# Delta-rule inverse: the first four levels on compact 32x32 blocks in four quarters of the array, the fifth as off-diagonal 32-row blocks

## The chip, the core and the metric

One core of a Trainium2 chip runs the whole program in one launch. The metric is device time in microseconds (us). TensorE is called PE in the profile (PEld is its weight load), VectorE DVE, ScalarE ACT, GpSimd POOL, and SyncE, which issues the weight transfers, SP.

## The reference, cut to what matters

The program is a stack of two model blocks over 256 tokens of width 1024: attention, feed-forward, a gated delta-rule layer (GDN), feed-forward, and then a second stack of feed-forward, convolution and pooling layers. The change touches only the GDN layer. For each of its 16 value heads, and each chunk of tokens, the reference solves a unit lower triangular system:

```
m = where(strict, beta[..., :, None] * kk * decay, 0.0)
a = m + eye(C)
sol = triangular_solve(a, rhs, left_side=True, lower=True, unit_diagonal=True)
```

The kernel works in chunks of 128 tokens, so there are two matrices of 128x128 for a head (t = 0 and 1), and it builds their explicit inverses by doubling: from 2x2 blocks on the diagonal to 4x4, 8x8, 16x16, 32x32, 64x64 and 128x128. With X the inverse so far and A the matrix, a level is the product A X, a mask that leaves the identity and the negated blocks below the diagonal, and two more products that apply X to it, one giving the next X and the other its transpose.

## The kernel before, in words

The 16 heads are taken in four turns (`N_TURNS`) of four heads (`GB`). Each engine has its own hand-written program, and they meet at semaphores. The inner order of a turn i is written out in `gdn_pe`: for each of the six levels, `level_pe(i, lv)` and then one or two fill tiles. A fill tile (`gdn_unit_pe`, one of twelve units of the next turn) is a 256-token projection of 24 matmuls, lines L519, L520 and L521, which need nothing of the level. `FILL` gives their number for the six levels: 2, 2, 1, 2, 1, 1. Unit x waits for the convolution of unit x-2 (`g_conv`) and for its own weights split into a high part (`split_hi` on ACT, L476) and a low part (`split_lo` on DVE, L483). The split of unit x is done three units ahead. In the last turn there are no next units, and the fill is one output projection a level (`gdn_out_pe`, L1253, no convolution to wait for).

A level has, for t = 0 and 1: the product p (L1335; L1332 in level 5), the mask on DVE (`level_dve`, L1839; a plain negation, L1835, in level 5), the product xi (L1350), the product ix (L1361; L1358 in level 5), and ACT copies of xi and ix to SBUF (`level_act`, L1576 and L1580; L1583 at level 4, L1586 at level 5). PE issues p for both t, then xi and ix for t = 0, then xi and ix for t = 1. Every block is 64x64 on one of two row halves (`HALVES`), so one t has 4 heads x 2 halves = 8 matmuls. In the trace a float32 matmul has two records, one behind the other in the program, each with a weight load of its own, so such a group of 8 matmuls is 16 records. The two halves use different tiles of the array, rows and columns 0 to 63 and rows and columns 64 to 127. At level 4 xi is done for the upper half alone, and at level 5 p and ix are one tile each.

DVE runs, behind the two masks of a level: the decay arguments (L1771) at level 0; the three taps of the convolution of units 0 and 1 (`taps_conv_dve`, L1747) with a weight split behind each at level 1; the taps of units 2 and 3 and then a split at level 2; a split, the taps of unit 4, a table and a split at level 3; the taps of units 5 and 6 and a split at level 4. ACT runs, behind the four copies of a level, the splits' high parts (L476), and at level 3 first the squares (`qk_squares_act`, L1536) on which PE's `qk_sums_pe` (L1263) waits between fill units 5 and 6.

Before level 0 the starting blocks are made: `unit_lower_dve` masks A into `xb` (L1807, one instruction a half), `pairs_turn_pe` transposes it on PE (L1313, 16 records for a t), and `pairs_act` copies it (L1569). In turn 0 this stands at the end of a prologue in which DVE is the busy engine. Masks and tables lie in `CONSTS`, loaded at the start by two SP transfers. `gdn_clear_dve` clears the lower left quarters of `xt_` on DVE (L1718). `gdn_pool` waits for the gates and sends them through DRAM.

Of the kernel before, what the change touches and what calls it, by code (L numbers as in the profile page):

```python
# [59 lines left out]
for _name, _n in COLS:  # L60
# [5 lines left out]
          ("level", 5 * 64), ("pair_t", 64), ("incl_up_neg", 128), ("strict_up", 128), ("reset", T), ("centre", 128), ("pool_inv", 4 * T)]  # L66
# [53 lines left out]
def build(nc, dram, out_dram):  # L120
    with ExitStack() as ctx:
# [1044 lines left out]
        g_beta = sem("beta_ready")  # L1166
# [31 lines left out]
        x_, ip, xb = gd.cut(2, GB, H), gd.cut(2, GB, H), gd.cut(2, GB, H)  # L1198
# [117 lines left out]
        def level_pe(pe, i, lv):  # L1316

            base = 2 * LEVELS * i + 2 * lv
            for t in range(2):
# [9 lines left out]
                for n in range(GB):  # L1329
                    o = slice(n * H, (n + 1) * H)  # L1330
                    if lv == LEVELS - 1:
                        last = nc.tensor.matmul(ps[HALVES[1], bank, o], a_t[HALVES[0], t, n, HALVES[1]], x_[HALVES[0], t, n], start=True, stop=True)  # L1332
                    else:
                        for r in HALVES:
                            last = nc.tensor.matmul(ps[r, bank, o], a_t[r, t, n, r], x_[r, t, n], start=True, stop=True)  # L1335
                last.then_inc(g_p, 1)
            for t in range(2):
# [9 lines left out]
                if lv < LEVELS - 1:  # L1347
                    for n in range(GB):
                        for r in HALVES[:1] if lv == LEVELS - 2 else HALVES:
                            last = nc.tensor.matmul(ps[r, level_bank(lv, "xi", t), n * H:(n + 1) * H], xb[r, t, n], ip[r, t, n], start=True, stop=True)  # L1350
# [4 lines left out]
                for n in range(GB):  # L1355
                    o = slice(n * H, (n + 1) * H)
                    if lv == LEVELS - 1:
                        last = nc.tensor.matmul(ps[HALVES[0], bank, o], ip[HALVES[1], t, n], xt_[HALVES[1], i % 2, t, n, HALVES[1]], start=True, stop=True)  # L1358
                    else:
                        for r in HALVES:  # L1360
                            last = nc.tensor.matmul(ps[r, bank, o], ip[r, t, n], xb[r, t, n], start=True, stop=True)  # L1361
# [205 lines left out]
        def pairs_act(act, i, t):  # L1567
            act.wait_ge(g_turned, 2 * i + t + 1)
            nc.scalar.activation(flat(x_[:, t]), ps[:, 2 + t, 0:T], ACT.Copy).then_inc(g_x0, 1)  # L1569

        def level_act(act, i, lv, t):
            base = 2 * LEVELS * i + 2 * lv + t + 1
            if lv < LEVELS - 1:
                act.wait_ge(g_xi, 2 * (LEVELS - 1) * i + 2 * lv + t + 1)
                r = HALVES[0] if lv == LEVELS - 2 else slice(0, P)
                nc.scalar.activation(flat(x_[r, t]), ps[r, level_bank(lv, "xi", t), 0:T], ACT.Copy).then_inc(g_x, 1)  # L1576
            act.wait_ge(g_ix, base)
            bank = level_bank(lv, "ix", t)
            if lv < LEVELS - 2:
                last = nc.scalar.activation(flat(xb[:, t]), ps[:, bank, 0:T], ACT.Copy)  # L1580
            elif lv == LEVELS - 2:
                for r in HALVES:
                    last = nc.scalar.activation(xt_[r, i % 2, t, :, r], ps[r, bank, 0:T].rearrange("p (n s) -> p n s", n=GB), ACT.Copy)  # L1583
            else:
                r = HALVES[0]
                last = nc.scalar.activation(xt_[r, i % 2, t, :, HALVES[1]], ps[r, bank, 0:T].rearrange("p (n s) -> p n s", n=GB), ACT.Copy)  # L1586
# [1115 lines left out]
```

## Time and profile before

| what | value |
|---|---|
| median of the runs | 1829.75 us (1829.43 to 1829.8, 3 runs) |
| span of the profiled execution | 1828.1 us, 1.65 us under the median |
| granted TensorE clock | 0.998 of full, mean over the span |
| PE busy | 1792.8 us, 98% |
| DVE busy / ACT busy | 1359.7 us, 74% / 1012.4 us, 55% |
| level loops of the four turns | 375 us to 622 us of the span |

The span is the time from the first to the last instruction; start and end of the launch lie around it. Starts are in us from the span's start. A duration in a matmul row includes the way through the array, so neighbouring matmuls overlap and it is the distance of starts that tells the rate: for n records in a merged row it is about (duration of the row less one duration) / (n - 1).

### The profile page before, as it was taken

How to read it: one execution, taken by the hardware profiler on the slowest of the kernel's cores; microseconds unless marked ns; L12 is line 12 of the kernel's file. 1: busy time of each engine (PE TensorE's matmuls, PEld its weight loads, DVE VectorE, ACT ScalarE, POOL GpSimd, SP SyncE). 2: the span in 40 equal slices, each digit the busy share in tenths (PEclk: the TensorE clock that was granted, in tenths of full speed). 3: DMA queues.
4: the chain of work that ended last, by engine and by line, in shares of the span. 5: the costliest groups of instructions: out<-in, count | busy, mean ns of one | idle time of the engine just before them, and what ended most of it. 6: DMA issues, size and time to landing. Idle time of an engine off the chain costs nothing.

```text
span 1828.1 us, 30994 instructions
## 1 busy us (share of the span) xinstructions
PE 1792.8 (98%) x12370; PEld 1591.7 (87%) x12370; DVE 1359.7 (74%) x2255; ACT 1012.4 (55%) x1687; POOL 83.1 (5%) x161
## 2 busy tenths in 40 slices
PE   7999999999999999999999999999999999999998
PEld 6888889889888888888888888888888888988887
DVE  4758878876765048889888969598979897767665
ACT  3557754766665157664655421655556555466553
POOL 0000000000000000001000100010101010000000
PEclk9999999999999999999999999999999999999999
DMA  5256568433321256559788934588878887436552
GB/s 194 93 186 206 185 204 325 137 120 116 117 94 67 88 181 207 185 194 337 251 287 282 351 140 139 207 303 288 315 257 299 282 310 265 161 126 203 191 190 99
DMA packets 102814, 373.94 MB, mean 205 GB/s; under 512 B 11440, under 2 KB 11600, under 8 KB 102544
## 3 DMA queue, kind: packets, MB, share of 16 engines
q1 hardware_dynamic: 80352, 289.88, 46.0%
q0 software_dynamic: 22320, 82.09, 13.3%
q8 instruction: 98, 1.61, 0.4%
q14 instruction: 44, 0.36, 0.1%
HBM read 370.85 MB, written 1.08 MB: 203 GB/s over the span
## 4 chain that ended last, share of the span: by engine, by line
PE 93%; DVE 3%; ACT 3%; issue 1%; DMA 0%; SPq 0%; DVEq 0%; ACTq 0%
PE ps L512 39%; PE ps L515 21%; PE ps L1978 4%; PE ps L519 3%; PE ps L1253 3%; PE ps L520 3%; PE ps L521 3%; PE ps L603 2%; PE ps L890 2%; PE ps L2004 2%; PE ps L1075 1%; PE ps L1350 1%; PE ps L1361 1%; ACT weights_hi L476 1%; DVE weights_lo L483 1%
## 5 line engine op out<-in xcount | busy, mean ns | idle before, releaser
L483 DVE TENSOR_TENSOR weights_lo<-weight_ring,weights_hi 128x1024 fp32r<-128x1024 f32 x477 | 583.2, 1224 | 158.5 <-ACT weights_hi L476 157.6
L476 ACT ACTIVATE weights_hi<-weight_ring 128x1024 fp32r<-128x1024 f32 x477 | 500.9, 1055 | 196.5 <-PE ps L512 122.3
L512 PE MATMUL ps<-u_halves,weights_hi 128*128 128x512 f32 x2176 | 536.6, 391 | 2.3 <-DVE u_halves L379 1.8
L512 PEld LDWEIGHTS ps<-u_halves,weights_hi 128*128 128x128 f32 x2176 | 400.3, 188 | 83.5 <-DVE u_halves L379 3.4
L515 PE MATMUL ps<-u_halves,weights_lo 128*128 128x256 f32 x2176 | 304.4, 282 | 0.0
L515 PEld LDWEIGHTS ps<-u_halves,weights_lo 128*128 128x128 f32 x2176 | 288.1, 191 | 10.2
L512 PE MATMUL ps<-act_halves,weights_hi 128*128 128x512 f32 x952 | 231.6, 391 | 0.0
L512 PEld LDWEIGHTS ps<-act_halves,weights_hi 128*128 128x128 f32 x952 | 173.4, 188 | 32.8 <-DVE weights_lo L483 0.4
L713 DVE SCALAR_TENSOR_TENSOR ffn_tiles<-ffn_tiles,cond 128x1024 f32<-128x1024 f32 x144 | 175.4, 1220 | 3.5 <-DMA ffn_tiles<-in_ada 3.3
L625 ACT ACTIVATE ffn_tiles<-ps 128x512 f32<-128x512 f32 x136 | 80.8, 594 | 158.2 <-PE ps L515 158.1
L519 PE MATMUL ps<-u_halves,weights_hi 128*128 128x256 f32 x488 | 144.6, 296 | 8.1 <-DVE u L1747 6.1
L515 PEld LDWEIGHTS ps<-act_halves,weights_lo 128*128 128x128 f32 x1088 | 142.3, 191 | 6.4
L515 PE MATMUL ps<-act_halves,weights_lo 128*128 128x256 f32 x1088 | 145.8, 282 | 0.0
L688 DVE TENSOR_TENSOR ffn_tiles<-ps,ffn_tiles 128x512 f32<-128x512 f32 x136 | 93.9, 690 | 64.6 <-ACT ffn_tiles L625 64.5
L520 PE MATMUL ps<-u_halves,weights_hi 128*128 128x256 f32 x488 | 138.7, 284 | 0.0
L521 PE MATMUL ps<-u_halves,weights_lo 128*128 128x256 f32 x488 | 138.5, 284 | 0.0
L799 POOL DMA_DIRECT2D ffn_tiles<-in_ada x144 | 76.1, 529 | 1262.8 <-DVE ffn_tiles L713 798.8
L519 PEld LDWEIGHTS ps<-u_halves,weights_hi 128*128 128x128 f32 x488 | 93.9, 192 | 13.0 <-DVE u L1747 7.0
L260 ACT ACTIVATE u<-h 128x256 f32<-128x256 f32 x88 | 35.6, 411 | 107.6 <-DVE h L739 56.3
L520 PEld LDWEIGHTS ps<-u_halves,weights_hi 128*128 128x128 f32 x488 | 94.0, 193 | 1.1 <-issue 1.0
L521 PEld LDWEIGHTS ps<-u_halves,weights_lo 128*128 128x128 f32 x488 | 94.1, 193 | 0.0
L637 ACT ACTIVATE ffn_tiles<-ffn_tiles 128x256 f32<-128x256 f32 x136 | 56.2, 413 | 27.1 <-DVE ffn_tiles L696 11.8
(280 smaller groups left out, 2105.7 us busy)
## 6 DMA issues: line engine op xcount, KB each, us to landing
weight_ring<-in_w SPq DMA_DIRECT2D x545, 512.0 KB, 4.0
ffn_tiles<-in_ada POOLq DMA_DIRECT2D x144, 512.0 KB, 5.4
scaled<-gates_scratch POOLq DMA_DIRECT2D x8, 512.0 KB, 6.0
arena<-in_alibi POOLq DMA_DIRECT2D x1, 1536.0 KB, 7.1
h<-in_x SPq DMA_DIRECT2D x4, 256.0 KB, 3.9
out<-u SPq DMA_DIRECT2D x4, 256.0 KB, 2.1
consts<-in_consts SPq DMA_DIRECT2D x1, 704.0 KB, 9.8
cond<-in_cond SPq DMA_DIRECT2D x1, 512.0 KB, 10.5
```

The source lines that it names most:

```text
L476: nc.scalar.activation(w_slot(s)[0], ring[:, n % RING], ACT.Copy).then_inc(hi_ready, 1)
L483: nc.vector.tensor_tensor(lo, ring[:, n % RING], hi.bitcast(F32), ALU.subtract).then_inc(lo_ready, 1)
L512: return nc.tensor.matmul(ps[:, bank], hi, halves, start=start, stop=stop, skip_group_check=True)
L515: return nc.tensor.matmul(ps[:, bank, 0:T], lo, halves[:, 0], start=start, stop=stop, skip_group_check=True)
L519: nc.tensor.matmul(out, hi, halves[:, 0], start=start, stop=False)
L520: nc.tensor.matmul(out, hi, halves[:, 1], start=False, stop=False)
L521: return nc.tensor.matmul(out, lo, halves[:, 0], start=False, stop=stop)
L625: nc.scalar.activation(corr[:, f % 2], ps[:, b:b + 2, T:2 * T], ACT.Copy).then_inc(corr_ready, 1)
L688: nc.vector.tensor_tensor(gu[:, f % 3], ps[:, b:b + 2, 0:T], corr[:, f % 2], ALU.add).then_inc(gu_ready, 1)
L713: nc.vector.scalar_tensor_tensor(ada_ring[:, r], ada_ring[:, r], 1.0, cond[:], ALU.mult, ALU.mult, accum_out=mods[:, n:n + 1]).then_inc(ad ...
L799: pool.dma_start(ada_ring[:, n % 3], dram["ada"][n]).then_inc(ada_loaded[n % 3], 16)
L1978: last = nc.tensor.matmul(ps[:, n % 6, 0:T], ring[:, s, k], u[:, k], start=(k == 0), stop=(k == C - 1))
```

## The change

The first four levels (`SMALL`), which only ever fill 32x32 blocks on the diagonal, keep just these: four row quarters (`QUARTERS`) with 32 columns each. Matmuls are 32x32 on 32 columns, four to a head, each on its own quarter of rows and columns of the array. DVE masks and ACT copies of these levels work on 128x128 in place of 128x256. Level 3 has to write its results into the wider layouts, `x64` and `xt_`, quarter by quarter. Level 4 computes only the off-diagonal 32x32 blocks. Level 5 is as before, on the new names `x64` and `ip64`. The clearing goes from DVE to POOL and grows to all of `xt_` and `x64`. The constants shrink by 224 columns.

```diff
-          ("level", 5 * 64), ("pair_t", 64),
+          ("level", 4 * 32), ("pair_t", 32),
...
-        LEVELS, H = 6, 64
+        LEVELS, SMALL, H, Q = 6, 4, 64, 32
+        QUARTERS = tuple(slice(Q * q, Q * q + Q) for q in range(4))
+        UPPER_LOWER = ((QUARTERS[0], QUARTERS[1]), (QUARTERS[2], QUARTERS[3]))
...
 pairs_turn_pe:
-                for r in HALVES:
-                    last = nc.tensor.matmul(ps[r, 2 + t, n * H:(n + 1) * H], xb[r, t, n], ident[r, r], start=True, stop=True)
+                for r in QUARTERS:
+                    last = nc.tensor.matmul(ps[r, 2 + t, n * Q:(n + 1) * Q], xb[r, t, n], ident[r, r], start=True, stop=True)
...
 level_pe, product p:
+                    if lv < SMALL:
+                        for r in QUARTERS:
+                            last = nc.tensor.matmul(ps[r, bank, o], a_t[r, t, n, r], x_[r, t, n], start=True, stop=True)
+                    elif lv == SMALL:
+                        for r0, r1 in UPPER_LOWER:
+                            last = nc.tensor.matmul(ps[r1, bank, o], a_t[r0, t, n, r1], x64[r0, t, n, 0:Q], start=True, stop=True)
...
 level_pe, product xi:
+                        if lv < SMALL:
+                            for r in QUARTERS[:3] if lv == SMALL - 1 else QUARTERS:
+                                last = nc.tensor.matmul(ps[r, bank, o], xb[r, t, n], ip[r, t, n], start=True, stop=True)
+                        else:
+                            r = QUARTERS[1]
+                            last = nc.tensor.matmul(ps[r, bank, o], xt_[r, i % 2, t, n, r], ip[r, t, n], start=True, stop=True)
...
 level_pe, product ix:
+                    if lv < SMALL:
+                        for r in QUARTERS:
+                            last = nc.tensor.matmul(ps[r, bank, o], ip[r, t, n], xb[r, t, n], start=True, stop=True)
+                    elif lv == SMALL:
+                        for r0, r1 in UPPER_LOWER:
+                            last = nc.tensor.matmul(ps[r0, bank, o], ip[r1, t, n], xt_[r1, i % 2, t, n, r1], start=True, stop=True)
...
 level_act:
+            if i == 0 and lv == SMALL - 1 and t == 0:
+                act.wait_ge(g_cleared, 2)
+                if lv < SMALL - 1:
+                    last = nc.scalar.activation(flat(x_[:, t]), ps[:, bank, 0:GB * Q], ACT.Copy)
+                elif lv == SMALL - 1:
+                    for r in QUARTERS[0], QUARTERS[2]:
+                        nc.scalar.activation(x64[r, t, :, 0:Q], heads(r, bank), ACT.Copy)
+                    r = QUARTERS[1]
+                    last = nc.scalar.activation(x64[r, t, :, Q:H], heads(r, bank), ACT.Copy)
+                else:
+                    r = QUARTERS[1]
+                    last = nc.scalar.activation(x64[r, t, :, 0:Q], heads(r, bank), ACT.Copy)
...
+            if lv < SMALL - 1:
+                last = nc.scalar.activation(flat(xb[:, t]), ps[:, bank, 0:GB * Q], ACT.Copy)
+            elif lv == SMALL - 1:
+                for r in QUARTERS:
+                    last = nc.scalar.activation(xt_[r, i % 2, t, :, r], heads(r, bank), ACT.Copy)
+            elif lv == SMALL:
+                for r0, r1 in UPPER_LOWER:
+                    last = nc.scalar.activation(xt_[r0, i % 2, t, :, r1], heads(r0, bank), ACT.Copy)
...
 gdn_clear_dve:
-            for b in range(2):
-                nc.vector.memset(xt_[HALVES[1], b, :, :, HALVES[0]], 0.0)
...
 unit_lower_dve:
-            for r in HALVES:
-                mask = const("pair_t")[r].unsqueeze(1).to_broadcast([H, GB, H])
+            for r in QUARTERS:
+                mask = const("pair_t")[r].unsqueeze(1).to_broadcast([Q, GB, Q])
...
 level_dve:
+            if lv < SMALL:
+                mask = const("level", lv, Q).unsqueeze(1).to_broadcast([P, GB, Q])
+                src = ps[:, bank, 0:GB * Q].rearrange("p (n s) -> p n s", n=GB)
+                last = nc.vector.tensor_tensor(ip[:, t], src, mask, ALU.mult)
+            elif lv == SMALL:
+                for r0, r1 in UPPER_LOWER:
+                    last = nc.vector.tensor_scalar(flat(ip[r1, t]), ps[r1, bank, 0:GB * Q], -1.0, None, ALU.mult)
...
 gdn_pool:
+            pool.wait_ge(root_ready, 3)
+            nc.gpsimd.memset(xt_, 0.0).then_inc(g_cleared, 1)
+            nc.gpsimd.memset(x64, 0.0).then_inc(g_cleared, 1)
```

## Rows read from the trace of the kernel before

**Rows 1.** Windows by stage: busy time of each engine in one turn.

```profile
448.00:518.00 70.00, 68.43 (x910) 62.43 (x907) 47.94 (x85) 45.45 (x82) 1.04 (x2) 1.00 0.34 109
```

**Rows 2.** Waits, 375 to 666 us: who waited for whom, total, times, longest.

```profile
PE ps L519 <- DVE u L1747: 3.2, 3, 1.1
...
PE ps L1350 <- DVE arena L1839: 2.4, 3, 1.9
```

**Rows 3.** Instructions by form, 375 to 622 us: count, busy, mean ns.

```profile
L1839 DVE TENSOR_TENSOR arena<-ps,consts 128x256 f32<-128x256 f32 x40 | 16.7, 424 | 64.7 <-PE ps L1335 64.0
...
L1816 DVE TENSOR_TENSOR arena<-ps,arena 128x512 f32<-128x512 f32 x3 | 2.1, 687 | 0.0
```

**Rows 4.** Timeline of PE, level 1 of turn 1: start, duration.

```profile
455.42 1.15 PE L1335 MATMUL ps<-arena 64*64 64x64 f32 x32
456.63 0.68 PE L1350 MATMUL ps<-arena 64*64 64x64 f32 x16
...
458.64 0.39 PE L519 MATMUL ps<-u_halves,weights_hi 128*128 128x256 f32 x1
```

**Rows 5.** Timeline of DVE, level 1 of turn 1.

```profile
456.15 0.89 DVE L1839 TENSOR_TENSOR arena<-ps,consts 128x256 f32<-128x256 f32 x2 [6.32 <-PE ps L1335]
456.96 1.51 DVE L1747 SCALAR_TENSOR_TENSOR u<-ps,cols,u 128x253 f32<-128x253 f32 x3
460.12 1.23 DVE L483 TENSOR_TENSOR weights_lo<-weight_ring,weights_hi 128x1024 fp32r<-128x1024 f32 x1 [1.66 <-ACT weights_hi L476]
```

**Rows 6.** Timeline of PE, second fill unit of level 1.

```profile
462.83 0.39 PE L519 MATMUL ps<-u_halves,weights_hi 128*128 128x256 f32 x1 [1.06 <-DVE u L1747]
```

**Rows 7.** Timeline of ACT in turn 1: levels 1 and 3, scaled copies behind level 5.

```profile
458.76 0.38 ACT L1580 ACTIVATE arena<-ps 128x256 f32<-128x256 f32 x1
459.04 1.05 ACT L476 ACTIVATE weights_hi<-weight_ring 128x1024 fp32r<-128x1024 f32 x1
...
475.78 1.05 ACT L1536 ACTIVATE gdn_tiles<-mix 128x1024 f32<-128x1024 f32 x1
...
496.40 2.18 ACT L1563 ACTIVATE arena<-ps,arena 128x128 f32<-128x128 f32 x8
```

**Rows 8.** Timeline of PE, levels 4 and 5 of turn 1.

```profile
484.24 0.62 PE L1350 MATMUL ps<-arena 64*64 64x64 f32 x7
484.64 0.27 PE L1361 MATMUL ps<-arena 64*64 64x64 f32 x1
484.70 0.22 PE L1350 MATMUL ps<-arena 64*64 64x64 f32 x1
...
489.31 1.14 PE L1332 MATMUL ps<-arena 64*64 64x64 f32 x16
```

**Rows 9.** Timeline of PE, what of this line runs at 455.43.

```profile
455.42 0.27 PE L1335 MATMUL ps<-arena 64*64 64x64 f32 x2
```

**Rows 10.** Timeline, level 0 of turn 1.

```profile
446.09 1.15 PE L1335 MATMUL ps<-arena 64*64 64x64 f32 x32
446.99 0.75 DVE L1839 TENSOR_TENSOR arena<-ps,consts 128x256 f32<-128x256 f32 x2
```

**Rows 11.** Timeline of PE, level 3 of turn 1.

```profile
472.17 0.33 PE L1335 MATMUL ps<-arena 64*64 64x64 f32 x4
...
478.36 1.88 PE L1263 MATMUL ps<-gdn_tiles,consts 128*128 128x512 f32 x4
```

**Rows 12.** Timeline, end of the prologue, level 0 of turn 0.

```profile
376.52 1.22 DVE L483 TENSOR_TENSOR weights_lo<-weight_ring,weights_hi 128x1024 fp32r<-128x1024 f32 x1 [0.36 <-ACT weights_hi L476]
377.66 0.75 DVE L1839 TENSOR_TENSOR arena<-ps,consts 128x256 f32<-128x256 f32 x2
...
378.13 0.68 PE L1350 MATMUL ps<-arena 64*64 64x64 f32 x16 [1.93 <-DVE arena L1839]
```

**Rows 13.** Timeline of PE, the fill of level 1 in the last turn.

```profile
594.85 3.72 PE L1253 MATMUL ps<-mix,weight_ring 128*128 128x256 f32 x16
```

**Rows 14.** The page, part 3: packets, MB, share of 16 engines.

```profile
q8 instruction: 98, 1.61, 0.4%
```

More of the change, by code:

```diff
@@ L1347, in level_pe @@
                 if lv < LEVELS - 1:
+                    bank = level_bank(lv, "xi", t)
                     for n in range(GB):
-                        for r in HALVES[:1] if lv == LEVELS - 2 else HALVES:
-                            last = nc.tensor.matmul(ps[r, level_bank(lv, "xi", t), n * H:(n + 1) * H], xb[r, t, n], ip[r, t, n], start=True, stop=True)
+                        o = slice(n * Q, (n + 1) * Q)
+                        if lv < SMALL:
[4 more added lines that the diff above has]
+                            last = nc.tensor.matmul(ps[r, bank, o], xt_[r, i % 2, t, n, r], ip[r, t, n], start=True, stop=True)
                     last.then_inc(g_xi, 1)
@@ L1355, in level_pe @@
                 for n in range(GB):
-                    o = slice(n * H, (n + 1) * H)
-                    if lv == LEVELS - 1:
-                        last = nc.tensor.matmul(ps[HALVES[0], bank, o], ip[HALVES[1], t, n], xt_[HALVES[1], i % 2, t, n, HALVES[1]], start=True, stop=True)
-                    else:
-                        for r in HALVES:
-                            last = nc.tensor.matmul(ps[r, bank, o], ip[r, t, n], xb[r, t, n], start=True, stop=True)
+                    o, o64 = slice(n * Q, (n + 1) * Q), slice(n * H, (n + 1) * H)
+                    if lv < SMALL:
[4 more added lines that the diff above has]
+                            last = nc.tensor.matmul(ps[r0, bank, o], ip[r1, t, n], xt_[r1, i % 2, t, n, r1], start=True, stop=True)
+                    else:
+                        last = nc.tensor.matmul(ps[HALVES[0], bank, o64], ip64[HALVES[1], t, n], xt_[HALVES[1], i % 2, t, n, HALVES[1]], start=True, stop=True)
                 last.then_inc(g_ix, 1)
@@ L1577, in level_act @@
+                last.then_inc(g_x, 1)
             act.wait_ge(g_ix, base)
             bank = level_bank(lv, "ix", t)
[L1579 to L1583, printed above, removed]
-            else:
-                r = HALVES[0]
-                last = nc.scalar.activation(xt_[r, i % 2, t, :, HALVES[1]], ps[r, bank, 0:T].rearrange("p (n s) -> p n s", n=GB), ACT.Copy)
+            if lv < SMALL - 1:
[6 more added lines that the diff above has]
+                    last = nc.scalar.activation(xt_[r0, i % 2, t, :, r1], heads(r0, bank), ACT.Copy)
+            else:
+                last = nc.scalar.activation(xt_[HALVES[0], i % 2, t, :, HALVES[1]], heads(HALVES[0], bank, H), ACT.Copy)
@@ L2649, in constant_matrices @@
     put("window_mask", mask)
-    p, q = i % 64, j[:, 0:64]
-    for lv in range(5):
+    p, q = i % 32, j[:, 0:32]
+    for lv in range(4):
         z = 2 ** (lv + 1)
         below = (p // (2 * z) == q // (2 * z)) & (p // z % 2 == 1) & (q // z % 2 == 0)
-        a = CONST["level"][0] + 64 * lv
-        out[:, a:a + 64] = (p == q) * 1.0 - below
+        a = CONST["level"][0] + 32 * lv
+        out[:, a:a + 32] = (p == q) * 1.0 - below
     put("pair_t", (p == q) * 1.0 - ((q == p + 1) & (p % 2 == 0)))
```

29 lines of the change are left out of this document (12 added, 17 removed).

## The prediction

> **What bounds the kernel now.** I read the page first, then the waits of the GDN stretch, then the timelines of one turn, engine by engine. The page gives PE as busy for 98% of the span, and in a turn of 70 us it is busy 68.4 us, with DVE at 47.9 and ACT at 45.5 [rows 1]. PE's own waits are small: 3.2 us in all for the convolution and 2.4 us for a mask [rows 2], while DVE waits 64 us for product p [rows 3]. So time taken from PE's level work comes off the end, as far as the engines that now wait for PE are ready sooner too. That second half decides the size, so I go through the levels by the wait that ends last.
>
> Level 1 of turn 1, with T = 455.42 for its first product [rows 4]: p for both t, 32 records, ends its starts near T+0.93. The masks start at T+0.73 [rows 5]. xi starts at T+1.21, and four groups of 16 records later the fill starts at T+3.22 [rows 4]. The fill does not run free: its second unit waits 1.06 us for the taps of unit 1 and starts at 462.83 [rows 6]. Those taps stand behind a weight split on DVE that starts at 460.12 because it waited for ACT [rows 5], and ACT's L476 starts at 459.04, behind the last level copy at 458.76 [rows 7]. This is a chain from PE's last level product through ACT and DVE back to PE.
>
> **The price of a record.** (1.15 - 0.22) / 31 = 30 ns between starts with two halves in use [rows 4], in the steady part 29. With one tile in use (level 5) it is (1.14 - 0.22) / 15 = 61 ns, 58 without the longer first gap [rows 8]. So the halves really overlap, and each tile is bound by itself. Two records of the two halves start within 10 ns [rows 9], although the program has both records of a matmul one behind the other: the second half's first record passes the first half's second. At level 4 a record of L1361 starts at 484.64, before the last of L1350 at 484.70 [rows 8]; it also passes the two L1361 records of the busy tile. So PE looks past at least three matmuls and the loads between them, not much further: in the seven records before it did not.
>
> A 32x32 record on 32 columns takes about half of 58 ns on its tile, say 32 with the fixed part. A group of one t is now 4 heads x 4 quarters x 2 = 32 records. If all four quarters overlap, a record costs 32/4 = 8 ns; if the look-ahead reaches only three, 32/3 = 10.6. I take 9.5, so a group costs 0.30 us in place of 0.466. The bounds outside are 16 ns (two at a time, 0.51 us a group) and today's 29 ns a record (0.93 us).
>
> **Masks and copies.** 128x256 takes 424 ns and 128x512 687 [rows 3], so 128 columns less save 0.13: a mask takes 0.29. ACT copies of 128 columns start 0.254 us apart ((2.18 - 0.40) / 7) [rows 7], and I take this for 32-row copies as well; between 0.2 and today's 0.38 lies the unknown.
>
> **Level by level**, gain in the start of what follows. Today's first product is complete 0.05 ahead of its mask, at T+0.68; with the group 0.16 shorter it is complete at T+0.51, the mask starts at T+0.56, xi at T+0.91, four groups of 0.30 end, and the fill could start at T+2.25, 0.97 sooner.
> Level 0: DVE comes late anyway, with the mask at T+0.90 [rows 10], so xi gains only 0.13, the groups 0.65: 0.78.
> Level 1: the last product is 0.99 sooner, ACT's last copy 0.11 shorter, and the chain above moves whole: 1.10.
> Level 2: the fill unit needs the taps that follow the masks. The second mask starts 0.30 behind the first, the taps 0.21 behind that (0.34 today, less the 0.13), and three of them take 1.51 [rows 5]: they end at T+0.56+0.30+0.21+1.51 = T+2.58, and with the 0.05 that a semaphore takes the fill starts at T+2.63, not 2.25: 0.59. Here the convolution becomes the bound.
> Level 3: four copies become 14. They start at T+1.43 and take 14 x 0.254 = 3.56, then the squares 1.05 [rows 7], and PE's sums can start at T+6.04. Today they start at 478.36 - 472.17 = 6.19 [rows 11], bound by PE. Gain 0.15 of the 0.97: ACT takes the rest.
> Level 4: two tiles, 16 records at 16 ns, two short DVE instructions a t in place of one. PE alone would gain 0.96, the taps of unit 5 end at T+2.82, gain 0.34.
> Level 5: unchanged. The turned pairs: 2 x (0.466 - 0.304) = 0.32; L1807 becomes four instructions of the new mask's 0.29 where two of the old mask's 0.42 stood, 0.33 us a t, and in turns 1 to 3 fill units hide it.
> A turn in the middle: 0.78 + 1.10 + 0.59 + 0.15 + 0.34 + 0.32 = 3.28, twice 6.56. Turn 0: at the end of the prologue PE waits 1.93 us for the mask [rows 12], DVE gets 0.66 us more of L1807, of which its own wait of 0.36 for ACT takes up about 0.3. So the mask starts 0.35 later, ends 0.13 sooner than that, and with groups 0.65 shorter level 0 gains 0.42 there, and the turn 2.92. The last turn has no convolution: 4 x 0.97 + 0.96 = 4.84, since its fill of 3.65 us from T+2.25 [rows 13] covers the 14 copies, which end at T+4.99. Sum: 2.92 + 6.56 + 4.84 = 14.3 us.
>
> The rest I cost at nothing. The cleared tiles leave DVE where it then waits for ACT anyway. POOL's memsets lie ahead of its wait for the gates; if they were slow, the gate rows would come later, and the decay arguments of turn 0 wait for those. The masks' transfer gets smaller, behind the first weights. Level 4's and level 5's change of tile size has fills between, as now. Behind the GDN layer PE is the bound again and everything shifts along. The sum comes from one execution of 1828.1 us; the 1.65 us to the median stay. 1829.75 - 14.3 = 1815.4.
>
> The Trainium skill speaks against this change in one place: "TensorEngine Tiling (Array Packing)", Instruction Overhead, gives each matmul some 60 cycles whatever its columns, and says not to take a tiling factor from a dimension that is already small. By that floor of 25 ns a record a group would cost 0.80 us, near the slow bound. The pair that starts within 10 ns [rows 9] doesn't obey it across tiles; whether a long row of records does, no row shows.
> A second page, "TensorE: Matmul & The Clock Gate", section "Part 3: Packing small matmuls — row/col tiling", holds matmuls to program order. Then a quarter's two records would always wait for each other and a group would cost 16 x 32 ns = 0.51, the bound of two at a time. The record that passes three others [rows 8] says otherwise, at least for two tiles.
>
> **Rivals.** (1) All overlaps perfect, the copies short: groups of 0.25 give 17.1 us, and with ACT at 0.2 us a copy another 2.5: 1810 to 1813. It is the good end of the forecast.
> (2) Two at a time: 0.51 a group. Fill starts at T+3.3, level 3 loses 0.32 to ACT, level 4 keeps 0.34, the last turn gains 0.6. Sum within 1 us of nothing: 1829.5. For it: only two tiles are ever seen at once in the trace. Against: the record that passes.
> (3) The slower side: PE can't issue a load and a matmul in less than the 29 ns of today's steady row, whatever the tile. The records of levels 0 to 3 double, a group costs 0.93 us. The masks wait, xi starts at T+1.92, the fill at T+5.80, 2.58 later, four levels and the pairs give 11 us a turn: 44 us, 1874. It decides from 16 ns a record upward, since there the groups cost what they cost now. For it: 29 ns is the fastest long row in the trace. Against: one tile alone takes exactly twice that, so it looks like the tiles' own time, and pairs start within 10 ns.
> (4) The program text. A turn's small matmuls grow from 528 to 928 records, 51 KB more instructions. The instruction queue moved 98 packets of 16 KB in the span, each (0.4% x 16 x 1828 / 98) 1.2 us long [rows 14]. A level's 384 instructions would then be used in about 2 us, faster than a packet and its latency follow. If half of 16 levels lose 1 us and half of that is hidden, 4 us: 1819 to 1825.
>
> **How the numbers follow.** Forecast with its good end (1810 to 1820) 0.58, with stalls of the fourth kind or quarters that overlap less (to 1826) 0.12, two at a time 0.14, slower 0.16. Within 0.2% (3.7 us) is about what a measurement can't tell from no change. That gives faster 0.70, same 0.14, slower 0.16. The range 1810 to 1832 holds the first three; the forecast's own is 1810 to 1820.
>
> **What would show it.** The groups L1335, L1350 and L1361 of levels 0 to 3 with 32 records in 0.25 to 0.34 us plus one duration; four records that start within 30 ns. Level 2's fill waiting for L1747; PE's sums at level 3 starting about T+6.0, right behind the squares, with ACT's 14 copies 0.25 apart. The last turn's levels shorter by 1 us each, level 5 as before. Wrong it would be if a group takes 0.5 us or more, if the copies of 32 rows cost as much as today's (then 1.7 us more a turn, three times), or if PE stands idle inside a group.

## The result, and the profile after

The change made the kernel slower, by 7.3 us. Four runs of each on one chip: 1836.86 us (1834.63 to 1838.73) after, 1829.59 us (1828.03 to 1829.8) before, ratio 1.0040 with an interval of 1.0028 to 1.0052. The forecast was 1815.4. The profiled execution took 1834.63 us, its span is 1832.8, and the mean granted clock of TensorE is 0.992, where it was 0.998.

The windows of the four turns, to hold against [rows 1]. PE's busy time fell by 4.5 us in the second of them, but its idle time is in the fall too, and the turns didn't get shorter: from level 0 of turn 1 to level 0 of the last turn it is 140.6 us (447.63 to 588.21), before 138.7 (446.09 to 584.76). The eighth value of a row (behind POOL) is PE's granted clock, which was 1.00 in every such window before:

```profile
378.00:448.00 70.00, 63.26 (x1121) 57.23 (x1121) 42.95 (x77) 41.11 (x84) 1.05 (x2) 0.93 0.31 103
448.00:518.00 70.00, 63.97 (x1312) 57.45 (x1301) 47.27 (x89) 45.28 (x90) 1.05 (x2) 0.98 0.34 107
518.00:588.00 70.00, 63.70 (x1250) 57.72 (x1238) 44.13 (x86) 42.45 (x87) 0.00 (x0) 0.95 0.23 80
588.00:660.00 72.00, 66.84 (x1115) 57.11 (x1115) 8.67 (x18) 19.83 (x44) 0.00 (x0) 0.98 0.28 89
```

The waits of PE, 378 to 660 us, against [rows 2]. "issue" is time for which the profile shows nothing that PE waited for; before there was none of it here. Left out is a row of 1.0 us for masks:

```profile
PE ps L1371 <- issue: 7.4, 3, 3.0
PE ps L519 <- DVE u L1775: 5.2, 8, 1.0
PE ps L1359 <- issue: 4.7, 3, 1.9
PE ps L1362 <- DVE arena L1867: 1.8, 4, 0.4
PE ps L1266 <- ACT gdn_tiles L1551: 1.6, 2, 1.3
...
PE ps L520 <- issue: 0.6, 1, 0.6
```

A level without such a stall, level 0 of the last turn. p (L1336, both t) has 64 records in 0.75 us, xi and ix 32 each, one group about 0.28 behind the other, and the fill (L1256) starts 2.14 us behind p's start; before it was 584.76 to 587.98, 3.22 us:

```profile
588.21 0.75 PE L1336 MATMUL ps<-arena 32*32 32x32 f32 x64
589.08 0.45 PE L1359 MATMUL ps<-arena 32*32 32x32 f32 x32
589.36 0.46 PE L1371 MATMUL ps<-arena 32*32 32x32 f32 x31
...
590.35 0.48 PE L1256 MATMUL ps<-mix,weight_ring 128*128 128x256 f32 x1
```

And level 2 of turn 1. In the middle of xi of t = 1, behind 20 of its 32 records, PE stands for 1.65 us; the number in brackets is the idle time before a row. Level 1 of turn 1, with T = 456.07, has none:

```profile
465.74 0.75 PE L1336 MATMUL ps<-arena 32*32 32x32 f32 x64
...
467.22 0.38 PE L1359 MATMUL ps<-arena 32*32 32x32 f32 x20
469.24 0.28 PE L1359 MATMUL ps<-arena 32*32 32x32 f32 x10 [1.65 <-issue]
```

```profile
456.07 0.75 PE L1336 MATMUL ps<-arena 32*32 32x32 f32 x64
...
458.66 0.39 PE L519 MATMUL ps<-u_halves,weights_hi 128*128 128x256 f32 x1 [0.22 <-DVE u L1775]
```

Windows behind four of PE's idle stretches. The first lies behind the stall above, the second behind one of 2.70 us that ends at 545.9, the third behind one of 2.98 us that ends at 606.3, the fourth 1.2 us behind the end of PE's wait of 0.95 us in level 4 of turn 0. The clock of all four is 0.50, 1.2 GHz, and PE is busy throughout:

```profile
469.80:473.00 3.20, 3.20 (x18) 3.20 (x16) 1.23 (x1) 2.86 (x6) 0.00 (x0) 0.50 0.03 8
545.90:551.50 5.60, 5.60 (x32) 5.54 (x33) 3.05 (x3) 4.66 (x8) 0.00 (x0) 0.50 0.02 6
606.30:609.50 3.20, 3.20 (x21) 2.60 (x22) 0.00 (x0) 0.28 (x1) 0.00 (x0) 0.50 0.02 5
418.60:421.80 3.20, 3.20 (x17) 3.19 (x15) 1.33 (x2) 1.93 (x3) 0.00 (x0) 0.50 0.27 97
```

The page, part 3, against [rows 14]: 12 packets of instructions more. The trace has 28341 instructions of PE and PEld, which at 256 to a packet (e4_rates below) are 110.7 packets, so this queue carries PE's program text:

```profile
q8 instruction: 110, 1.80, 0.4%
```

So two costs stand beside the gain. PE's idle time under "issue" is 7.4 + 4.7 + 0.6 = 12.7 us, all but 0.6 of it inside the dense groups. The lower clock takes about (0.07 x 70 + 0.02 x 70 + 0.05 x 70 + 0.02 x 72) = 11.2 us of full-speed time. With the forecast gain of 14.3 they would give 9.6 us slower; the medians differ by 7.3, and the two profiled executions, from which these numbers are, by 4.7.

The trace has the text's packets one by one, and they can be held against the stalls. In the 2.34 us from 466.90 to the end of the stall above, one packet moves on all queues, and it is one of PE's text:

```profile
DMA packets 1, 0.02 MB, mean 7 GB/s; under 512 B 0, under 2 KB 0, under 8 KB 0
q8 instruction: 1, 0.02, 2.4%
```

It starts at 466.95 and takes 0.91 us; PE had crossed the border before at 465.90, ran dry at 467.60 and went on at 469.24, 2.29 us behind the packet's start. Counting PE's and PEld's instructions in the order of the trace gives 110 borders of 256 for 110 packets. At all seven stalls the packet started 2.2 to 2.6 us before PE went on. At the borders without a stall it started at least 2.2 us before PE came there, at most of them over 3: the border in level 1 of turn 1 at 457.74 has its packet at 455.22.

### The profile page after: what moved, and what is told of

Its sections match the earlier page's. It is cut to its first block, busy times and chain, and to the rows that moved or that the text cites. A ratio compares the mean times of both kernels' runs of the same rounds, so it can differ in the third digit from the quotient of the medians.

```text
span 1832.8 us, 34259 instructions
## 1 busy us (share of the span) xinstructions
PE 1777.1 (97%) x13970; PEld 1575.2 (86%) x13970; DVE 1358.6 (74%) x2277; ACT 1012.8 (55%) x1727; POOL 85.3 (5%) x163
## 3 DMA queue, kind: packets, MB, share of 16 engines
HBM read 370.74 MB, written 1.08 MB: 203 GB/s over the span
## 4 chain that ended last, share of the span: by engine, by line
PE 89%; DVE 5%; ACT 3%; issue 2%; DVEq 0%; DMA 0%; SPq 0%; ACTq 0%
PE ps L512 39%; PE ps L515 21%; PE ps L1256 3%; PE ps L519 3%; PE ps L520 3%; PE ps L521 3%; PE ps L603 2%; PE ps L890 2%; PE ps L2013 2%; PE ps L2039 2%; PE ps L1075 1%; DVE arena L2127 1%; DVE weights_lo L483 1%; ACT weights_hi L476 1%; DVE u L1775 1%
## 5 line engine op out<-in xcount | busy, mean ns | idle before, releaser
L512 PEld LDWEIGHTS ps<-u_halves,weights_hi 128*128 128x128 f32 x2176 | 400.3, 188 | 83.4 <-DVE u_halves L379 3.4
L519 PE MATMUL ps<-u_halves,weights_hi 128*128 128x256 f32 x488 | 147.7, 303 | 10.1 <-DVE u L1775 8.1
L520 PE MATMUL ps<-u_halves,weights_hi 128*128 128x256 f32 x488 | 141.7, 290 | 0.6 <-issue 0.6
L519 PEld LDWEIGHTS ps<-u_halves,weights_hi 128*128 128x128 f32 x488 | 97.0, 199 | 14.8 <-DVE u L1775 9.5
L520 PEld LDWEIGHTS ps<-u_halves,weights_hi 128*128 128x128 f32 x488 | 97.2, 199 | 1.9 <-issue 1.8
L637 ACT ACTIVATE ffn_tiles<-ffn_tiles 128x256 f32<-128x256 f32 x136 | 56.1, 413 | 27.1 <-DVE ffn_tiles L696 11.8
```

The source lines that it names most:

```text
L512: return nc.tensor.matmul(ps[:, bank], hi, halves, start=start, stop=stop, skip_group_check=True)
L519: nc.tensor.matmul(out, hi, halves[:, 0], start=start, stop=False)
L520: nc.tensor.matmul(out, hi, halves[:, 1], start=False, stop=False)
L637: nc.scalar.activation(sgb[:, f % 2], src, ACT.Silu).then_inc(sg_ready, 1)
```

## The experiments

Three theories. (1) PE uses up its program text faster than the text arrives: it stands at the border of a block of instructions, and the idle time then brings the clock down. (2) The stalls are waits of the level's own, for masks, copies or banks. (3) The thin matmuls bring the clock down by themselves. Each ratio below is to the kernel before, run beside it on the same chip.

**Shifting the text: e1_half and e1_whole.** Ahead of the delta rule, where PE's program has its norm sums:

```diff
+            if k == 2:
+                for n in range(32):                        # 64 in e1_whole
+                    r = slice(32 * (n % 4), 32 * (n % 4) + 32)
+                    nc.tensor.matmul(ps[r, 6, 0:32], ident[r, r], consts[r, 0:32], start=True, stop=True)
```

> The kernel after, with 32 more small matmuls (32x32 by 32, four quarters, into an unused bank) on TensorE where the norm ahead of the delta rule is summed: half a block of 256 instructions, nothing else. Theory 1 (the engine waits for its program text at the borders of 256-instruction blocks): the stalls of 0.9 to 3.2 us that the kernel after has at 384.2, 396.0, 467.4, 477.6, 543.0, 595.5 and 603.1 us leave those places and come back about half a block away, in other lines; their sum may be anything from 5 to 18 us, the time from 1829 to 1840 us. Theory 2 (waits of the inverse's own, for masks, copies or banks): the stalls stay in the same lines of the same levels with the same sizes within 0.3 us, and the time is that of the kernel after within 1 us (1836 to 1838).

> The same with 64 more small matmuls, which is one whole block of 256 instructions. Theory 1: the borders fall on the same instructions of the inverse as in the kernel after, so the stalls are in the same lines, with the same sizes within some 0.5 us, and the time is that of the kernel after plus at most 0.6 us: 1836.5 to 1838.5. Theory 2: the same places as well, so that this run alone tells nothing and is the control for the half block. If adding instructions ahead did something by itself, this run and the half block would both differ from the kernel after.

Half a block: 1844.74 us, ratio 1.0082 (1.0065 to 1.0099). A whole one: 1839.82 us, 1.0047 (1.0030 to 1.0064). The whole block's time stands above the 1836.5 to 1838.5 that I expected, with runs from 1834.51 to 1841.71, but its ratio agrees with the kernel after's 1.0040. In e1_whole (L1363 is xi, all lines 4 further) all seven stalls are back in their places. The same level breaks at the same record as in the kernel after, 20 in front and 10 behind:

```profile
470.87 0.38 PE L1363 MATMUL ps<-arena 32*32 32x32 f32 x20
472.62 0.37 PE L1363 MATMUL ps<-arena 32*32 32x32 f32 x10 [1.37 <-issue]
```

In e1_half that level has no break. The longer breaks of this turn stand in level 0, inside ix of t = 1 (L1375), and in a fill unit behind level 1 (L525), which has no mask, copy or bank of a level to wait for:

```profile
454.02 0.41 PE L1375 MATMUL ps<-arena 32*32 32x32 f32 x23
456.20 0.26 PE L1375 MATMUL ps<-arena 32*32 32x32 f32 x8 [1.78 <-issue]
...
468.28 0.28 PE L525 MATMUL ps<-u_halves,weights_lo 128*128 128x256 f32 x1 [1.01 <-issue]
```

The place of a stall follows the position in the text, so theory 2 is out for them. The count makes it sharper: in the kernel after, e1_half, e1_whole, e2_spread, e4_rates, e7_spread2, e9_spread3 and e10_dense there are 58 "issue" gaps of PE over 0.2 us, and every one stands at the same place within a block of 256, instruction 193 or 194 of the count. The kernel before and the variants of it without a row of small matmuls in levels 0 to 3 (e3_level4, e5_idle, e6_swap, e8_control, e11_level4) have none. Half a block of position is worth about 5 us of 1840: "issue" is 15.2 us in e1_half and 12.7 in e1_whole, and the clock from 375 to 666 us is 0.93 and 0.96.

**The price by itself: e4_rates.** The kernel before with float32 matmuls appended behind PE's last work:

```diff
+            warm_pe(6, 6)
+            for n in range(32):                            # then n % 2, then quarter[0], then 64x64 halves
+                r = quarter[n % 4]
+                nc.tensor.matmul(ps[r, 6, 0:32], ident[r, r], consts[r, 0:32], start=True, stop=True)
...
+            for n in range(512):                           # 2048 instructions
+                r = quarter[n % 4]
+                nc.tensor.matmul(ps[r, 6, 0:32], ident[r, r], consts[r, 0:32], start=True, stop=True)
```

> The kernel before with matmuls appended behind TensorE's last work, float32, in an unused bank, between warm-up matmuls: 32 of 32x32 over four quarters, over two, over one, 32 of 64x64 over the halves; then 512 of 32x32 over four quarters in a row (2048 instructions, eight blocks of 256), 256 of 64x64 (1024 instructions), and 32 groups of 8 matmuls of 32x32 with one of 128x256 behind each. Two records a matmul. Theory 1: short groups run at 9 ns a record over four quarters and 29 ns over halves, and the long one doesn't: it goes at the rate at which blocks arrive, about 3.4 us each, 26 ns a record and 27 us in all, in steps at the blocks' borders; the 64x64 ones take 15 us, just under that rate; the mixed ones (about 1.1 us for 36 instructions) show no step. Rival: the long group keeps 9 ns a record, 9 us in all, and the stalls in the kernel after have another cause.

The timeline of the short groups, 64 records each: 32x32 on four, two and one quarters, then 64x64 on halves. Less the last record of about 0.2 us, these are 9, 16, 32 and 29 ns a record:

```profile
1824.72 0.75 PE L2365 MATMUL ps<-consts 32*32 32x32 f32 x64
...
1828.19 1.20 PE L2369 MATMUL ps<-consts 32*32 32x32 f32 x64
...
1832.11 2.21 PE L2373 MATMUL ps<-consts 32*32 32x32 f32 x64
...
1837.04 2.08 PE L2377 MATMUL ps<-consts 64*64 64x64 f32 x64
```

The long row over four quarters. It runs through its first 255 records and then stops behind every 128, which are 256 instructions, a packet of 16 KB:

```profile
1844.42 2.34 PE L2381 MATMUL ps<-consts 32*32 32x32 f32 x255
1848.88 1.27 PE L2381 MATMUL ps<-consts 32*32 32x32 f32 x128 [2.12 <-issue]
1852.35 1.93 PE L2381 MATMUL ps<-consts 32*32 32x32 f32 x128 [2.20 <-issue]
1856.09 1.93 PE L2381 MATMUL ps<-consts 32*32 32x32 f32 x128 [1.82 <-issue]
```

From block to block it takes 3.47 to 3.75 us, whether the records take 1.27 us at full or 1.93 at half clock, which came behind the first stop. The time has three parts: the next block's packet starts 1.03 to 1.16 us behind a border, takes 0.89 to 1.18 us, and PE goes on 1.28 to 1.55 us behind its end. No other engine works meanwhile:

```profile
1852.35:1870.20 17.85, 9.63 (x640) 8.96 (x640) 0.00 (x0) 0.00 (x0) 0.00 (x0) 0.50 0.02 5
```

All 1024 records take 26 us, 25 ns a record; theory 1 said 27, its rival 9. The 64x64 row has no stop:

```profile
1877.67 15.15 PE L2385 MATMUL ps<-consts 64*64 64x64 f32 x512
```

That is 3.8 us for 256 instructions, just above what the text needs. The kernel before had such matmuls and no stall. The groups of 16 records with a 128x256 matmul behind each (36 instructions in 0.88 us) ran without a stop too.

The Trainium skill, "Runtime: NRT & Kernel Launch", section "Instruction fetch mechanics", calls the crossing of such a block mostly hidden and gives the engine's own issue rate as the reason. This case's trace agrees for the 64x64 row, at 15.15 / 1024 = 14.8 ns an instruction, and disagrees for the 32x32 row, at 4.5 ns, where 1.5 to 2.2 us of every block show.

**Idle time without thin matmuls: e5_idle.** The kernel before; PE waits in levels 0 and 2 of each turn for a chain of memsets on POOL:

```diff
+            if lv in (0, 2):
+                pe.wait_ge(g_delay, 7 * i + (2 if lv == 0 else 7))
             for t in range(2):
                 pe.wait_ge(g_ip, base + t + 1)
```

> The kernel before, in which TensorE waits once in level 0 and once in level 2 of each turn, between the p products and the rest, for a chain of 2 and 5 memsets on GpSimd (about 1 and 2.4 us): no instruction of TensorE is added, its matmuls stay 64 wide. It is the idle time of the kernel after without its thin matmuls. If idle time itself is what the clock answers with (theory 1): the granted clock is at its lower level for a stretch behind several of the eight waits, above all the longer ones; the time is that of before plus 10 to 14 us of waits plus 7 to 14 us for half clock: 1847 to 1857, granted clock 0.985 to 0.992. If the thin matmuls themselves bring the lower clock (theory 3): the clock stays at 0.998 and the time is 1840 to 1844.

1847.23 us (1845.24 and 1849.22), ratio 1.0106 (1.0088 to 1.0125): 19.4 us more. The eight waits are 16.4 us, 14.0 more than the waits for masks that stood there [rows 2]. The first long wait, then the windows behind the first and the third:

```profile
397.60 0.62 PE L1353 MATMUL ps<-arena 64*64 64x64 f32 x13 [2.75 <-POOL arena L1961]
```

```profile
398.30:401.60 3.30, 3.30 (x52) 3.18 (x49) 0.00 (x0) 1.95 (x5) 0.00 (x0) 0.50 0.00 0
...
546.50:560.00 13.50, 13.44 (x217) 12.07 (x218) 9.15 (x13) 9.89 (x18) 0.00 (x0) 1.00 0.25 81
```

Three of the four waits of 2.75 us were followed by half clock (at 398.3, 473.4 and 613.6), the third was not, and none of the four short ones. The matmuls are the 64-wide ones of before. So idle time alone can do it, and theory 3 isn't needed; e7_spread2 below, with the thin matmuls and full clock, speaks against it. The time is at the low edge of what I expected, and the clock, 0.997 and 0.994, above it: three stretches of some 3.3 us account for 5 us, the waits for the other 14.

**Level 4 alone: e3_level4.** The kernel before, with only the 32-to-64 level changed:

```diff
-                    if lv == LEVELS - 1:
+                    if lv == LEVELS - 2:
+                        for r0, r1 in UPPER_LOWER:
+                            last = nc.tensor.matmul(ps[r1, bank, n * Q:(n + 1) * Q], a_t[r0, t, n, r1], x_[r0, t, n, 0:Q], start=True, stop=True)
+                    elif lv == LEVELS - 1:
```

> The kernel before with one part of the change: the 32-to-64 level computes only the two off-diagonal 32-row blocks; the first four levels stay on 64x64 halves. Prediction's step for this level: 0.34 us a turn on TensorE plus nothing else: 1828.2, with a range of 1826 to 1829.5. Theory 1: the text is not longer than before, no stall appears at a block's border, the granted clock stays at 0.998, and the time is under that of before by 1 to 2.5 us. A rival, that the off-diagonal level's own waits (copies of quarters on ScalarE, 1.1 us for the taps of unit 5) cost more than they save: 1830 to 1834.

1831.69 us, ratio 1.0010 (1.0000 to 1.0020): the rival. No stall for text, but PE now waits for convolutions six times and not three, 6.0 us where it was 3.2 [rows 2]; and behind the wait of level 4 in turn 1 comes half clock:

```profile
PE ps L519 <- DVE u L1765: 6.0, 6, 1.1
```

```profile
488.00:491.40 3.40, 3.40 (x19) 3.40 (x18) 1.63 (x3) 2.25 (x4) 0.00 (x0) 0.50 0.19 55
```

**What idle time of PE is worth: e6_swap.** The kernel before, one swap on DVE in level 1:

```diff
                         taps_conv_dve(dve, steps, i + 1, 0)
-                        gdn_lo_dve(dve, i + 1, 0)
                         taps_conv_dve(dve, steps, i + 1, 1)
+                        gdn_lo_dve(dve, i + 1, 0)
                         gdn_lo_dve(dve, i + 1, 1)
```

> The kernel before with one pair of VectorE operations swapped in level 1 of the turns: the convolution of unit 1 goes ahead of the low part of unit 0's split. It takes away TensorE's wait of 1.33 us for that convolution, three times. If TensorE's idle time in the turns is what counts at the end: 1825.6 to 1828 (up to 4 us less than before). If the wait only moves (to the low part for unit 3): 1829 to 1830. It doesn't tell the main theories apart, it says what a microsecond of TensorE's idle time in a turn is worth.

1823.49 us against 1827.85, ratio 0.9980 (0.9970 to 0.9989): 4.4 us less (2.0 to 5.5 by the interval) for 3.2 us of waits, whose row is gone. PE's time comes off the end in full, as far as the interval can tell.

**Level 4 again, with its convolution ready: e11_level4.** e3_level4 with the swap, ScalarE's squares ahead of level 3, and the tap and convolution of unit 5 ahead of level 4:

```diff
                         silu_conv_act(act, i + 1, 4)
+                        tap_act(act, i + 1, 5)
                         ln_exp_tables(act)
...
                         gdn_lo_dve(dve, i + 1, 4)
+                        taps_conv_dve(dve, steps, i + 1, 5)
                     elif more and lv == 4:
-                        taps_conv_dve(dve, steps, i + 1, 5)
```

> The kernel before with only the 32-to-64 level on off-diagonal 32-row blocks, and with the swap, the squares ahead of level 3 and the tap and convolution of unit 5 before level 4. Alone, that level gained 1.2 us of TensorE's time a turn and lost it to a wait of 1.15 us for the convolution of unit 5 and to the half clock behind it. If that is the cause: no wait and no half clock here, 1818.5 to 1821, under the swap kernel's 1823.5. If the level's own copies and masks cost the gain: 1823 to 1825.

1819.54 us, ratio 0.9948 (0.9930 to 0.9966). Behind turn 0's first mask PE's longest wait in the turns is 0.4 us, the clock 1.00 throughout. Level 4 of turn 1 takes 2.28 us from p to its fill, before 3.22: 0.94 gained, where the prediction gave PE alone 0.96. It is there once the convolution is:

```profile
476.71 0.69 PE L1334 MATMUL ps<-arena 32*32 32x32 f32 x32
...
478.99 0.39 PE L519 MATMUL ps<-u_halves,weights_hi 128*128 128x256 f32 x1
```

Four turns give 3.8 us. The median is 3.9 under e6_swap's, but that one was measured on another chip, and here the squares are moved too.

**Spreading the text: e2_spread, e7_spread2, e9_spread3.** The kernel after; the fill units are cut in eighths and put between a level's dense groups, so that 128 instructions in 0.6 us are followed by 1 us of a unit:

```diff
+        PLAN = [([], [], [(0, 0, 8), (1, 0, 2)]),
+                ([(1, 2, 5)], [(1, 5, 8)], [(2, 0, 8), (3, 0, 2)]),
...
             for t in range(2):
+                between(t)
                 pe.wait_ge(g_ip, base + t + 1)
```

> The kernel after with the same matmuls in another order on TensorE: each level's three dense groups of 32-row matmuls have 2 to 4 eighths of a fill unit between them, so that 128 instructions in 0.6 us are followed by a stretch of 18 to 24 instructions in 1 us. Theory 1: no stall over 0.5 us is left at the borders of the blocks, which gives back the 14 us of them, and the 24 us at half clock, worth about 10 us of work, go with the idle time that preceded them: 1812 us, down to 1806 if the units also fill the waits for the masks (about 1 us a level). Theory 2 (own waits): the waits are moved, not taken away: 1828 to 1836. Theory 3 (the half clock comes of the thin matmuls themselves, not of the stalls): the stalls go and the granted clock stays at 0.99: 1820 to 1824.

1829.7 us, ratio 1.0006 (0.9991 to 1.0022), with ten runs from 1825.57 at a clock of 0.999 to 1836.22 at 0.993. Less than I expected: 9.4 us of "issue" waits are left in the profiled run, one of them 2.5 us long in a fill unit, and the window from 485.8 to 499.2 behind it stands at 0.50. The waits of its own stayed: 3.4 us for the convolution and 2.2 for ScalarE's squares. The run-to-run spread goes with the clock: the work is the same.

e7_spread2 has the swap of e6_swap and the squares ahead of level 3 besides.

> The spread order of the kernel after (fill units in eighths between the dense groups) with two more moves: the swap on VectorE, and ScalarE's squares ahead of level 3 rather than behind its copies, since the spread kernel's profile shows waits of 1.4 us for the convolution and 2.0 us for the sums. Theory 1: these go (about 5 to 8 us over four turns), the remaining stalls at the blocks' borders (1.2 to 2.7 us, 7 us in the profiled run) stay or grow, since less idle time stands between blocks, and runs differ among themselves with the number of half-clock stretches: a median of 1822 to 1827. If the waits were what bounds it and the text nothing: 1815 to 1819 and no stall.

1816.57 us, ratio 0.9943 (0.9930 to 0.9957): faster than both kernels, and the lowest median of the case, though its interval overlaps e11_level4's. "issue" waits are down to 3.4 us, and the clock is 1.00 in all four windows with the thin matmuls in them, so these don't bring it down by themselves.

```profile
PE ps L1372 <- DVE arena L1878: 3.0, 4, 1.0
PE ps L519 <- DVE u L1789: 2.6, 3, 0.9
PE ps L1348 <- issue: 2.1, 3, 0.9
PE ps L1384 <- issue: 1.3, 3, 0.8
```

e9_spread3 also has the tap of unit 5 earlier.

> The second spread kernel with one more move: ScalarE applies the tap of unit 5 ahead of its table load and root in level 3, so that the convolution of unit 5 is done before TensorE wants unit 7 in level 4 (a wait of 1.06 us a turn in that kernel's profile). If idle time of TensorE comes back in full: 3 us less, 1813 to 1814.5. If a stall for text takes its place, since the blocks then follow one another sooner: 1815 to 1817.

1820.86 us, ratio 0.9951 (0.9930 to 0.9972), a miss. The wait for unit 7 is gone, and a wait of the same length stands one level on, at level 5's ix, because DVE reaches that level's mask later than PE does; behind it PE has half clock (485.0 to 488.3 at 0.50):

```profile
482.67 0.67 PE L1389 MATMUL ps<-arena 64*64 64x64 f32 x8 [0.97 <-DVE arena L1886]
```

**The controls: e8_control and e10_dense.** The first is e9_spread3's order and moves on the kernel before, the second the same moves on the kernel after in its own order, with the convolution of unit 5 earlier on DVE as well.

> The control for the two spread kernels: the kernel before, with its 64-wide matmuls, in the same spread order, with the same moves (the swap on VectorE, the squares ahead of level 3, and the tap of unit 5 ahead of ScalarE's root). If the spread order and the moves did it all and the 32-row blocks nothing: 1814 to 1817, as good as the spread kernels. If the order only serves to thin out the short matmuls' instructions (theory 1): the swap's gain and little else, 1821 to 1823.5, so that the 32-row blocks are worth 6 to 8 us once their text arrives in time.

> The kernel after in its own dense order, with the swap, the squares ahead of level 3 and the tap and convolution of unit 5 before level 4: every wait of its own that its profile shows is attended to, the stalls at the blocks' borders are not. Theory 1: they remain, 1 to 3 us each, some seven to nine of them, with half clock behind several: 1824 to 1832, at least 7 us above the spread kernel with the same moves. Theory 2 (own waits did it): 1814 to 1818.

e8_control: 1837.34 us, 1.0040 (1.0025 to 1.0054), much slower than I expected of either theory. Its clock is 1.00. The spread order costs 13.9 us against e6_swap: PE waits 4.0 us for masks, where e6_swap has 0.4, and from a unit's last matmul to a group's first it is 0.21 us from start to start (458.09 to 458.30), where the unit's own are 0.12 apart. So the order is a price, and e9_spread3, in the same order, is 16.5 us under it. That is what the 32-row blocks are worth in this order, when most of their text arrives in time. It isn't what they are worth at best: e11_level4, with 64-wide matmuls in levels 0 to 3, comes to 0.9948 in the old order, against e7_spread2's 0.9943. The intervals overlap, so no run shows that 32-row blocks in levels 0 to 3 add anything to level 4 and the moves.

e10_dense: 1827.41 us, 1.0000 (0.9988 to 1.0012), 10.8 above e7_spread2 and 6.6 above e9_spread3, whose moves are nearer its own; I had expected at least 7. Its own waits are nearly gone. Six of the seven stalls are where they were in the kernel after, and with a new one of 0.3 us they make 12.3 us:

```profile
PE ps L1371 <- issue: 7.5, 3, 3.0
PE ps L1359 <- issue: 3.7, 3, 1.8
...
PE ps L520 <- issue: 1.1, 1, 1.1
```

## Why the prediction was wrong

The step that failed is the program text, which the forecast's sum leaves out. I had it as rival 4, with the right place ("a level's 384 instructions would then be used in about 2 us, faster than a packet and its latency follow") and the wrong size: 4 us, from "half of 16 levels lose 1 us and half of that is hidden". It measured 12.7 us, seven stalls with a mean of 1.8 us, and I can find none of it hidden: PE was the bound, and its idle time comes off or goes on the end in full (e6_swap). The working held a part of the number: a packet of about 1.2 us [rows 14]. What it lacked was the time from one block to the next, 3.5 us in e4_rates, of which the packet is a third. The second half of the failure is the clock, which the prediction doesn't mention at all: about 11 us.

Point by point:
- **The price of a record** was right, and was the step I doubted most. 0.30 us a group was forecast, 0.28 measured (589.08 to 589.36); 9 ns a record over four quarters in e4_rates. The rivals with 16 and 29 ns a record are out, the latter as a price of the engine; as a price of the text, 25 ns a record over a long row, it came back.
- **The two rules of the Trainium skill** that spoke against the change fail on these rows. The floor of the page "TensorEngine Tiling (Array Packing)", section "Instruction Overhead", doesn't hold across tiles: 9 ns a record. That e4_rates' long row has its 25 ns comes of the blocks, since it stops only there. And the program order of "TensorE: Matmul & The Clock Gate", "Part 3: Packing small matmuls — row/col tiling", would give two at a time, 16 ns.
- **Masks**: 0.29 forecast, 0.29 measured (L1864, mean 290 ns).
- **Copies of 32 rows**: 0.254 apart forecast, 0.28 measured; (1.11 - 0.27) / 3 in the row below. At level 3 of turn 1 (p at 474.29) the squares start at T+5.34, not T+4.99, and PE's sums at T+6.46 and not T+6.04: 0.27 lost against before, where I had 0.15 gained.

```profile
475.67 0.55 ACT L1598 ACTIVATE arena<-ps 32x128 f32<-32x128 f32 x2 [0.80 <-PE ps L1359]
...
476.52 1.11 ACT L1611 ACTIVATE arena<-ps 32x128 f32<-32x128 f32 x4
...
479.63 1.06 ACT L1551 ACTIVATE gdn_tiles<-mix 128x1024 f32<-128x1024 f32 x1
```

- **Levels**: where no stall falls, PE did what was forecast. Level 0 of the last turn gained 1.08 (forecast 0.97), level 0 of turn 1 0.88 (0.78): its fill starts 2.50 us behind p, before it was 446.09 to 449.47. Level 1 of turn 1 gained 0.81 and not 1.10 where its chain ends: the second fill unit starts at 462.67, T+6.60, before T+7.41. Its first fill gained 0.63, since it starts at T+2.59, waiting for the taps. That is the bound that I worked out for level 2 (T+2.63) and forgot for level 1.
- **Level 4** of turn 1 lost 0.09 (485.53 to 488.84, 3.31 us; before 483.03 to 486.25, 3.22) where I had 0.34 gained. Four DVE instructions stand ahead of the taps of unit 5 (1.22 us, 486.02 to 487.27), and the fill waits 0.96. e11_level4 shows that without this wait, behind which e3_level4 had half clock in turn 1, the level has its gain.
- **The sum of 14.3 us** is not refuted: in equal order the 32-row blocks gave 16.5 us (e8_control to e9_spread3), although e9_spread3 waits longer for masks (5.9 us against 4.0) and has stretches at half clock. For the kernel after itself an estimate closes the account. From the shorter groups PE's own work should be 16 levels x 6 groups x (0.466 - 0.28) = 17.9 us less, level 4 gives 4 x 0.94 = 3.8 and the turned pairs 1.5, 23.2 in all. Against it stand 12.7 us of stalls, about 11.2 of clock, and 6.2 more of PE's other waits in the turns (11.8, before 5.6): 6.9 us slower, between the 4.7 of the profiled executions and the 7.3 of the medians.

Settled are the place of the stalls (position in the text, e1 and the count), the time of a block (e4_rates), that idle time can bring half clock (e5_idle), and level 4 (e3, e11). A border passes without a stall where its packet has started some 2.2 to 2.5 us or more before PE comes. Open stays why some packets start ahead of the border before theirs and others only 0.6 to 2.5 us behind it, and why 2.75 us of idle time brought half clock three times in four. I didn't try fewer instructions with 32-row blocks, for instance in one t alone.

## What to carry to other kernels

Splitting a matmul into smaller tiles multiplies instructions while it shortens each; divide the instructions of the densest stretch by its time, and where that is under about 14 ns an instruction (3.5 us / 256) for 256 in a row, reckon with 3.5 us a block and not with the engine's rate, and look in the trace for when the packets start. A wait of 0.95 us on TensorE can be followed by 3.2 us at half clock, 1.6 us of full-speed time, so a short new wait can cost well over twice its length. Spread dense groups over slow work only after pricing each change of tile size (0.21 us from start to start here, in place of 0.12). Change one part at a time: level 4 with its convolution moved gave nearly what the whole change gave at its best. Before a wait is moved, ask what is next on the engine that releases it: e9_spread3 took one away and got it back one level on.

## What was unexpected of the hardware

- In an unbroken row of short matmuls TensorE's text arrives at 3.47 to 3.75 us per 256 instructions, nearly three times the 1.2 us of the packet; PE goes on 2.2 to 2.7 us behind the packet's start. The same stop is seen with all other engines at rest (DMA share 0.02), so no contention is needed for it.
- Behind idle stretches of 1.0 (level 4) to 3.0 us the granted clock was at 1.2 GHz for stretches of 3.2 to 13.4 us, with the engine busy again. Behind others of the same length it wasn't: a wait of 1.54 us ahead of turn 0 was followed by it in the kernel before (0.53 from 342.0 to 345.3) and not in the kernel after.
- Four quarters give 9 ns a record, two 16, one 32: tiles overlap almost without loss as long as the text is there.
- 128 instructions' worth of text position, with 64 records of work less, moved the kernel by 5 us (1839.82 to 1844.74).
